# Key rows by VectorE's 32x32 transposes and inverse softmax sums by one transposing product per tile

## What is computed

```python
q, k, v, lf, u, p = project(xp, w_in[l], b_forget[l])
att = fox_prompt(q, k, v, lf).reshape(bp, n_prompt, D_ATT)
...
# in fox_prompt, for one block of 128 query rows
s = jnp.einsum('bqhd,bkhd->bhqk', qi, kp, preferred_element_type=jnp.float32) * SCALE
s = s + ci.transpose(0, 2, 1)[..., None] - cum_k
pr = jax.nn.softmax(jnp.where(mask, s, NEG_INF), axis=-1)
return jnp.einsum('bhqk,bkhd->bqhd', pr.astype(vp.dtype), vp)
...
kp_l.append(k)      # returned as k_prompt: a row per token, 512 floats
kq_l.append(k)      # returned as k_sample
```

## Time and profile before

| | us |
|---|---|
| runs of the kernel before | 998.30, 1002.22, 1003.92 |
| their median | 1002.22 |
| profiled execution, from its first to its last instruction | 996.7 |
| the attention phase within it | about 206.9 to 496.5 |

### The profile page before, as it was taken

How to read it: one execution, slowest core, us unless ns; L and a number is a source line. 1 busy time by engine, 2 the same in 40 slices (tenths; PEclk the granted TensorE clock), 3 DMA queues, 4 the chain that set the end, 5 groups by cost and what they waited for, 6 DMA issues and landing times. The chain is left out here.

```text
span 996.7 us, 13885 instructions
## 1 busy us (share of the span) xinstructions
PE 915.8 (92%) x5085; PEld 582.6 (58%) x5085; DVE 433.9 (44%) x1309; ACT 322.1 (32%) x652; POOL 213.4 (21%) x299
## 2 busy tenths in 40 slices
PE   4999999999999999998799999996799999999785
PEld 4655645555556665566554454443788787878431
DVE  4689799613444344446533326648000100001157
ACT  6751515613233333335423234331212121111223
POOL 3088000012002147741011000422000000000155
PEclk9999999999999999999999999997799999999988
DMA  9540000454983016317342121466967888967294
GB/s 231 164 173 1 2 0 2 139 189 140 421 351 109 1 66 212 127 43 275 111 168 58 42 72 45 169 263 228 304 224 252 307 317 271 379 234 265 85 385 156
DMA packets 63854, 173.89 MB, mean 174 GB/s; under 512 B 17432, under 2 KB 26703, under 8 KB 58279
## 3 DMA queue, kind: packets, MB, share of 16 engines
q1 hardware_dynamic: 55047, 141.37, 40.4%
q0 software_dynamic: 8544, 31.07, 8.6%
q10 hardware_dynamic: 192, 0.52, 0.2%
HBM read 113.76 MB, written 59.24 MB: 174 GB/s over the span
## 5 line engine op out<-in xcount | busy, mean ns | idle before, releaser
L2181 PE MATMUL banks<-arena,mixT 128*128 128x512 f32 x288 | 130.5, 599 | 0.0
L1492 PE MATMUL banks<-xT,arena 128*128 128x384 f32 (+1 forms) x384 | 123.8, 478 | 6.0 <-DVE mx L1703 4.1
L1492 PEld LDWEIGHTS banks<-xT,arena 128*128 128x128 f32 x384 | 71.4, 190 | 56.3 <-DVE mx L1703 11.5
L2181 PEld LDWEIGHTS banks<-arena,mixT 128*128 128x128 f32 x288 | 52.7, 192 | 55.4 <-issue 55.4
L1611 ACT ACTIVATE arena<-arena,mx 128x128 f32<-128x128 f32 (+8 forms) x72 | 58.5, 813 | 75.9 <-DVE mx L1703 75.4
L2348 PEld LDWEIGHTS banks<-mixT,v_tok 128*128 128x128 f32 x512 | 72.5, 195 | 4.5 <-issue 4.5
L2348 PEld LDWEIGHTS banks<-mixT,arena 128*128 128x128 f32 x512 | 70.4, 190 | 6.8 <-issue 6.8
L2348 PE MATMUL banks<-mixT,v_tok 128*128 128x160 f32 x512 | 73.1, 305 | 0.8 <-ACT mixT L2562 0.8
L2348 PE MATMUL banks<-mixT,arena 128*128 128x160 f32 x512 | 71.7, 300 | 0.8 <-ACT mixT L2562 0.8
L2719 POOL DMA_INDIRECT arena<-y_park,slot_s x18 | 17.1, 949 | 254.6 <-DMA y_park<-arena 249.4
L3011 DVE TENSOR_TENSOR mixT<-arena,banks 128x320 f32<-128x320 f32 x16 | 7.8, 488 | 129.8 <-PE banks L2348 129.8
(11 more groups left out here) (420 smaller groups left out, 1349.1 us busy)
## 6 DMA issues: line engine op xcount, KB each, us to landing
arena<-in_w_down SPq DMA_DIRECT2D x16, 1024.0 KB, 8.6
x_slots<-xT SPq DMA_DIRECT2D x4, 2048.0 KB, 13.9
y_park<-xT SPq DMA_DIRECT2D x4, 2048.0 KB, 30.4
v_tok<-in_w_gate SPq DMA_DIRECT2D x8, 1024.0 KB, 6.2
v_tok<-in_w_up SPq DMA_DIRECT2D x8, 1024.0 KB, 6.0
arena<-in_w_gate SPq DMA_DIRECT2D x8, 1024.0 KB, 4.9
arena<-in_w_up SPq DMA_DIRECT2D x8, 1024.0 KB, 7.2
arena<-x_slots SPq DMA_DIRECT2D x16, 512.0 KB, 5.3
```

The source lines that it names most:

```text
L1492: last = T.matmul(b[:, 0:cn], w[:, k, :], xT[:, k, c0:c0 + cn], start=(k == 0), stop=(k == KD - 1))
L2181: last = T.matmul(bank[half], mixT[:, k, t * P:(t + 1) * P], w_oh[half][:, k, :], start=(k == 0), stop=(k == KD - 1))
```

## The change

VectorE makes the key rows instead of TensorE. `turn_k`, ScalarE's `keys` and their waits are gone. VectorE's `keys` is now two instructions that transpose 32x32 blocks within each quarter of the partitions, from `kT` in SBUF to `k_tok` in SBUF: one over 1024 columns, one over the last 96. A block then holds 32 tokens by 32 columns, so SP stores a pair with twelve transfers (three for each quarter) in runs of 32 floats, 128 B. Their completion counts go from 64 to 256, and VectorE's `keys(i)` waits for the stores of the pair before.

For the inverse sums VectorE's `reciprocals` reads each sum 64 times and writes 512 numbers per partition for a group of four tiles (128 for group 2), so that TensorE can spread them with one transposition per tile in place of a product per tile and head. `rl` grows to 5x128 columns, groups 0 and 1 share a part, and VectorE waits until TensorE has read what stood there.

```diff
-            k_tok = gflat[:, 0:NT * P].rearrange("p (t n) -> p t n", t=NT)
+            KB = 8 * P // 32
+            LATE = TOK - 96
+            k_tok = gflat[:, 0:8 * P + 96].rearrange("p (b n) -> p b n", n=32)
...
-            rl = tmp("rl", [P, 2 * NT])
+            rl = tmp("rl", [P, 5 * P])
+            RL = (0, 0, 4 * P)
...
-                    sp.wait_ge(s_cp[0], k0)
-                    sp.wait_ge(s_cp[1], k1)
-                    sp.dma_start(kp[0:8 * P, cols].rearrange("(t p) n -> p t n", p=P), k_tok[:, 0:8, :]).then_inc(s_ko[0], 16)
-                    sp.dma_start(kp[8 * P:NPR, cols], k_tok[0:META, 8, :]).then_inc(s_ko[1], 16)
-                    sp.dma_start(ks[:, cols], k_tok[META:META + NSA, 8, :]).then_inc(s_ko[2], 16)
+                    sp.wait_ge(s_kt, i + 1)
+                    for a in range(4):
+                        cols = slice(i * P + 32 * a, i * P + 32 * a + 32)
+                        rows_ = slice(32 * a, 32 * a + 32)
+                        sp.dma_start(kp[0:8 * P, cols].rearrange("(b j) n -> j b n", j=32),
+                                     k_tok[rows_, 0:KB, :]).then_inc(s_ko[0], 16)
+                        sp.dma_start(kp[8 * P:NPR, cols],
+                                     k_tok[32 * a + 8 * P - LATE:32 * a + 32, KB, :]).then_inc(s_ko[1], 16)
+                        sp.dma_start(ks[:, cols].rearrange("(b j) n -> j b n", j=32),
+                                     k_tok[rows_, KB + 1:KB + 3, :]).then_inc(s_ko[2], 16)
...
                     for t in range(t0, t1):
                         q = nq(t)
-                        for h in range(2):
-                            last = T.matmul(b[HD * h:HD * h + HD, (t - t0) * P:(t - t0) * P + q],
-                                            rl[0:q, 2 * t + h:2 * t + h + 1].to_broadcast([q, HD]),
-                                            ident[0:q, 0:q], start=True, stop=True)
+                        last = T.transpose(b[:, (t - t0) * P:(t - t0) * P + q],
+                                           rl[0:q, RL[grp] + P * (t - t0):RL[grp] + P * (t - t0 + 1)],
+                                           ident[0:q, 0:q])
                     last.then_inc(s_T[0], 1)
...
-                turn_k(0)
                 scores(0, 0)
...
                     inverses(i, 1)
-                    if i < 3:
-                        turn_k(i + 1)
                     weigh(*waiting)
...
                 def keys(i):
-                    taken[0] += 1
-                    dve.wait_ge(s_T[1], taken[0])
+                    dve.wait_ge(s_free, of_rows[i, 2] + 1)
                     if i:
                         for s in s_ko:
-                            dve.wait_ge(s, 16 * i)
-                    V.tensor_copy(k_tok[:, 4:8, :], bank[5][:, :].rearrange("p (t n) -> p t n", t=4)).then_inc(s_cp[1], 1)
+                            dve.wait_ge(s, 64 * i)
+                    V.transpose(k_tok[:, 0:KB, :], kT[i % 2][:, 0:8 * P])
+                    V.transpose(k_tok[:, KB:KB + 3, :], kT[i % 2][:, LATE:TOK]).then_inc(s_kt, 1)
...
                     dve.wait_ge(s_ex, 2 * NT * i + 2 * t1)
-                    V.reciprocal(rl[0:q, 2 * t0:2 * t1], lsum[0:q, 2 * t0:2 * t1]).then_inc(s_rl, 1)
+                    if grp == 1:
+                        dve.wait_ge(s_T[0], inv_at[i, 0])
+                    elif i:
+                        dve.wait_ge(s_T[0], inv_at[i - 1, grp + 1 if grp == 0 else 2])
+                    V.reciprocal(rl[0:q, RL[grp]:RL[grp] + P * (t1 - t0)].rearrange("p (n d) -> p n d", d=HD),
+                                 lsum[0:q, 2 * t0:2 * t1].unsqueeze(2).to_broadcast([q, 2 * (t1 - t0), HD])
+                                 ).then_inc(s_rl, 1)
```

More of the change, by code:

```diff
@@ L1295, in hybrid_step @@
             inv_at = {}
-            c0_, c1_ = 2, 1
+            c0_, c1_ = 0, 0
             for i in range(4):
@@ L1306, in hybrid_step @@
                 inv_at[i, 1] = c0_
-                if i < 3:
-                    c0_, c1_ = c0_ + 2, c1_ + 1
                 c0_ += 1
@@ L1330, in hybrid_step @@
             s_out = sem("a_outputs")
+            s_kt = sem("a_keys_turned")
             s_ko = [sem(f"a_out_k{n}") for n in range(3)]
@@ L1425, in _ @@
                 for i in range(4):
-                    cols = slice(i * P, i * P + P)
-                    k0 = turned[i - 1, NT - 1, 0] + 3 if i else 2
-                    k1 = turned[i - 1, NT - 1, 1] + 1 if i else 1
-                    sp.wait_ge(s_cp[0], k0)
-                    sp.wait_ge(s_cp[1], k1)
-                    sp.dma_start(kp[0:8 * P, cols].rearrange("(t p) n -> p t n", p=P), k_tok[:, 0:8, :]).then_inc(s_ko[0], 16)
-                    sp.dma_start(kp[8 * P:NPR, cols], k_tok[0:META, 8, :]).then_inc(s_ko[1], 16)
-                    sp.dma_start(ks[:, cols], k_tok[META:META + NSA, 8, :]).then_inc(s_ko[2], 16)
+                    sp.wait_ge(s_kt, i + 1)
[8 more added lines that the diff above has]
+                                     k_tok[rows_, KB + 1:KB + 3, :]).then_inc(s_ko[2], 16)
                     if i >= 1 and i < 3:
@@ L1456, in _ @@
                 for s in s_ko:
-                    sp.wait_ge(s, 64)
+                    sp.wait_ge(s, 256)
                 sp.wait_ge(s_woa, 16)
@@ L1493, in project @@
                     last.then_inc(s_ring, 1)
[L1495 to L1503, removed]
                 def scores(i, t):
@@ L1612, in exps @@
                                  accum_out=lsum[0:q, 2 * t + h:2 * t + h + 1]).then_inc(s_ex, 1)
-                def keys(i):
-                    for g in (0, 2):
-                        taken[0] += 1
[L1617 to L1625, removed]
                 def inverses(i, grp):
@@ L1638, in turned_block @@
                     copy_turned(act, S.copy, 0, i, t, bl, u, taken[0])
-                keys(0)
                 exps(0, 0, 0)
@@ L1661, in _ @@
                     inverses(i, 1)
-                    if i < 3:
-                        keys(i + 1)
                     inverses(i, 2)
```

## The result

The kernel after takes 1012.51 us in the median of four runs (1006.4 to 1015.68). Against the kernel before (1000.26 in the median of its four runs) the ratio is 1.012, with a 95% interval of 1.008 to 1.016: some 12 us slower. The forecast was 1007.4 in a range of 1002 to 1013.5, with slower as the likelier sign. It was 5.2 us added to a median of 1002.22, that of the three times known then; a further 998.30 makes it 1000.26. So the time lies in the range, near its upper end, while the increase is more than twice the 5.2 us that were added up.

The account below looks back on a forecast made before the run. The prediction took TensorE (92% busy) as the bound, with GpSimd setting the pace in pair 2 up to tile 4. Terms 0 - 0.8 + 0 + 1.2 + 2.6 + 1.4 + 0.8 = +5.2 us gave 1007.4, range 1002 to 1013.5.

Parts of the forecast that it names:

- The reciprocal at 6.28 ns a column: VectorE's inverse sums: 512 columns take 3.37 us in place of 0.20, about 29 us more VectorE work in all.
- The plain pass for the transposition: VectorE's key block transpositions cost as much as a plain pass: 1.23 us for 1024 columns, 0.25 for 96.
- The ends of pairs: Ends of pairs 0 and 2: saved key transpositions and pauses offset the longer reciprocal, 0 each; pair 1's end doesn't count.
- the first rival: More TensorE pauses at pair ends and tile 4 of pair 2 bring half clock: +7 to +11.5 us, say 1011; chance 0.25.
- the signs that were to prove the prediction wrong: A reciprocal below 2 us, a GpSimd store wait well above today's, or granted clocks below 1 at pair ends.
- Tile 4 of pair 3: TensorE waits for the longer reciprocal: 3.0 us less 0.4 saved, +2.6; lowered clock behind it, +0.8 more.
- Tile 4 of pair 2: GpSimd has made VectorE late, so TensorE waits for the reciprocal: 1.6 us less 0.4 saved, +1.2.
- GpSimd sets the pace in pair 2: VectorE waits 3.04 us for GpSimd's masks up to tile 4; this lead covers what moves at pair 1's end.
- The stores: SP's twelve key stores of 128 B runs, about 16 us a pair at worst, are hidden: 0 us.
- the second rival: 128 B stores delay GpSimd's stores and loads in pair 2: +7 to +9 us, 1010; chance 0.08.
- Start of pair 0: VectorE's key transpositions are covered by ScalarE's first exponential; an earlier table load may gain 0.5: 0 (-0.5 to +0.5) us.

Follow-up runs that it names:

- the clock is held: Kernel after plus unread identity transpositions ahead of TensorE's wait for the inverse sums (28, 12, 14 a place), so TensorE works while waiting: ratio 1.0066 against the kernel before.
- when GpSimd's steps go: Kernel before with GpSimd's nine stream steps moved into tiles 4 to 8 of pair 1 and 4 to 7 of pair 2: ratio 0.9994.
- two other kernels: Kernel after with the old inverse sums (ratio 0.9994), and kernel before with its key stores split into twelve of 128 B runs (1.0054).
- the run with the load moved: Kernel after with the old inverse sums, and the 1040 KB mask-row load for pair 3 held until tile 6 of pair 2: ratio 0.9975 against the kernel before.
- small reciprocal and copy: Kernel after with the reciprocal of 8 (or 2) sums a row only, then a VectorE copy spreading them to 512 (128) columns: ratio 1.0011 against the kernel before.
- keys alone: Kernel after with inverse sums made and spread as in the kernel before, leaving only the key rows' change: ratio 0.9994 against the kernel before.
- the same kernel with GpSimd's later steps moved: Kernel after with the old inverse sums and GpSimd's nine stream steps moved out of pair 2's short tiles: 992.63 us, ratio 0.9940 against the kernel before.

## Why the forecast was right, and where not

- *Durations.* The reciprocal at 6.28 ns a column was right: 3347 / 512 = 6.5. The Trainium skill ("VectorE: DVE Perf Modes", First, the fixed hardware budget) gives the reciprocal a repeat count of 8, from which the prediction worked out an estimate of 4.3 us; the trace has 3.35, it doesn't agree, and the measurement decides. The plain pass for the transposition was right to 5 ns.
- *The ends of pairs* are the term that was mis-sized: 0 forecast, +6.3 measured. The balance of waits was right (-0.25 each once the clock is held); what failed is the step that put no half clock behind TensorE's pause there. The pause of 1.8 us stood in the first rival, at 1 us each and a quarter of the chance, and was set aside with the argument that the earlier trace rows show a fall only behind 2.17. No row showed a pause of 1.8 without a fall. Clocks below 1 at the ends of pairs were among the signs that were to prove the prediction wrong, and they came, at all three. So the sum came out at 5.2 for 11.3: the sign was right by the terms, the size by the rival, which gave 1011. That the time still lies in the stated range is owed to that rival's upper bound and to the higher median that the sum was added to.
- *Tile 4 of pair 3.* Right as a wait (+2.62 with the clock held, +2.6 forecast); the clock there cost 2.3, not 0.8. The start of the next phase cost another 1.4, which no term had: TensorE runs at half there in the kernel before too, but for longer after (0.64 and 0.50 from 506 to 510 and 510 to 514 us, where before has 0.66 and 0.92 from 495 to 499 and 499 to 503).
- *Tile 4 of pair 2.* +1.2 forecast, -0.96 measured, and both have their reason. With the waits filled VectorE waits 3.76 us for the mask of this place (3.31 before), and the place costs +1.36. In the kernel after pair 2 is 4.6 us late, VectorE waits 0.86 us for the mask, and its reciprocal lies beside TensorE's projection:

```profile
410.70 2.99 PE L1496 MATMUL banks<-xT,arena 128*128 128x336 f32 x10
411.53 3.35 DVE L1720 RECIPROCAL rl<-lsum 128x512 f32<-128x512 f32 x1
...
415.51 0.65 PE L1545 MATMUL banks<-ident,rl 128*128 128x128 f32 x4
```

- *GpSimd sets the pace in pair 2* was a wrong reading of the earlier trace rows. VectorE's 3.04 us, up to 390.52, lay beside a projection that TensorE needed anyway (the row below, from the timeline before), and the kernel before gains only 0.7 us at tile 4 when GpSimd's steps go. So the end of pair 1 was not covered (+2.78). GpSimd was a limit just ahead, which a gain upstream runs into.

```profile
386.82 5.43 PE L1492 MATMUL banks<-xT,arena 128*128 128x384 f32 x16
```

- *The stores* at 0 were right for the kernel after, by the luck of 3 us. GpSimd's longer waits for its stores, which the second rival feared, cost two other kernels 5.7 and 5.9 us between the first scores of tiles 5 and 6 of pair 2, but through the load that the twelve issues push back; for the first of them the run with the load moved shows that it was not the 128 B runs themselves.
- *Start of pair 0* gained 0.9, a little more than the 0.5 that the range allowed. The load of the exponentials' table, 1.28 us, stood at 238.58 before, right ahead of the first exponential; after it is at 208.47, while ScalarE waits.

## What to carry over

Do the dear operation on as few elements as there are and spread the result with a copy: the number of elements on the free axis sets the price of the reciprocal (some 6.5 ns a column here), not how many of them differ. Where a step makes the busiest engine wait, look at the granted clock behind the wait as well: here it cost 8.5 us, and the waits, less the change's gains, 2.8. And a gain ahead of another engine's fixed cadence is worth nothing, or less than nothing, until that engine's work is moved, so move both in one step.

## What the runs showed of the hardware

- How long TensorE pauses doesn't alone decide whether the clock falls: 1.16 us ahead of the spreading in tile 4 of pair 3 brought it to 0.57 (small reciprocal and copy), while 1.57 us in tile 4 of pair 2 (keys alone) left it at 1.00. Nor do the instructions: at the start of pair 0 TensorE has the same ones, with the same pauses of 0.73 and 1.10 us, in the keys' half alone and in the same kernel with GpSimd's later steps moved; behind them tile 2 ran at 0.50 in the first trace (240 to 242 us) and at 1.00 in the second (239 to 241). What it hangs on was not tried, and one trace of a kernel doesn't show where the clock falls in its other runs.
- Products that are thrown away kept the clock up and shortened the program: 28, 12 and 14 transpositions a place brought the kernel after from a span of 1011.0 us to one of 998.8 and from a ratio of 1.0121 to 1.0066, with intervals that overlap at the edge.
- A 128 KB store of 128 B runs lands in 2.2 us (median of 16; 3.8 for the four in pair 2), a 512 KB store of 512 B runs in 4.0; between 365 and 410 us the queue's row shows 1424 packets for 1.63 MB at 10.5% of the DMA engines' time before and 4880 packets for the same bytes at 17.4% after, 1.7 times the time a byte. The Trainium skill ("DMA: Bandwidth & Descriptors", Specifications) has it that runs under 512 B stay below line rate: the trace agrees, but the time was lost through the order of two transfers and not through bandwidth.
- A 1040 KB load issued 0.6 us ahead of a 512 KB store on another engine's queue held that store by 4 to 6 us (GpSimd waited 6.07 and 7.74 us in place of some 2); issued 3 us behind it, by nothing that the trace shows.
